# A VectorE product cut in two: when eight multiply-adds run in one piece behind two blocks' low parts

## What is computed

```python
def modulation(cvec, w_mod, b_mod):                  # cvec: 2048, w_mod: 2048 x 12288
    m = jax.nn.silu(cvec) @ w_mod + b_mod            # six vectors of 2048, for c and for c_ctx
    return m.reshape(cvec.shape[0], N_MOD, 1, D_MODEL)

def trunk_layer(x, mod, h0, g, w_in, ...):
    hn = rmsnorm(x, g[0]) * (1.0 + mod[:, 1]) + mod[:, 0]
    z = hn @ w_in                                    # 2048 x 5120
    ...                                              # RG-LRU heads, short convolutions
    x = x + mod[:, 2] * (m @ w_out)
    hn = rmsnorm(x, g[1]) * (1.0 + mod[:, 4]) + mod[:, 3]
    f = (jax.nn.silu(hn @ w_gate) * (hn @ w_up)) @ w_down
    return x + mod[:, 5] * f
```

## Time and profile before

| | before |
|---|---|
| time, median of 3 runs | 1750.77 us (1750.06 to 1751.92) |
| profiled execution, its own time | 1751.09 us |
| its span, first to last instruction | 1749.3 us |
| PE busy | 1710.8 us, 98% of the span |
| DVE busy | 945.4 us, 54% |
| ACT busy | 609.8 us, 35% |
| mean granted clock of PE | 0.992 |

### The profile page before, as it was taken

How to read it: one execution, slowest core, us unless ns; L and a number is a source line. 1 busy time by engine, 2 the same in 40 slices (tenths; PEclk the granted TensorE clock), 3 DMA queues, 4 the chain that set the end, 5 groups by cost and what they waited for, 6 DMA issues and landing times.

```text
span 1749.3 us, 24522 instructions
## 1 busy us (share of the span) xinstructions
PE 1710.8 (98%) x10063; PEld 1632.9 (93%) x10063; DVE 945.4 (54%) x1405; ACT 609.8 (35%) x701; POOL 63.3 (4%) x99
## 2 busy tenths in 40 slices
PE   5999999999999999999999999999999999999997
PEld 3678999999899979999999999999999999999997
DVE  4446678777778578343534434353534435353445
ACT  3333455456523253222222222323232222223235
POOL 2000100110010110000000000000000000000000
PEclk8999999999999999999999999999999999999999
DMA  9996655576677876343334333433333334333421
GB/s 362 379 358 223 239 207 199 201 239 206 212 241 268 289 254 228 121 134 132 120 120 135 129 120 121 136 127 120 121 136 127 120 123 137 124 120 122 141 74 73
DMA packets 206268, 307.56 MB, mean 176 GB/s; under 512 B 5500, under 2 KB 151216, under 8 KB 203776
## 3 DMA queue, kind: packets, MB, share of 16 engines
q1 hardware_dynamic: 189472, 237.07, 40.2%
q0 software_dynamic: 16528, 69.63, 11.1%
q10 hardware_dynamic: 208, 0.02, 0.0%
HBM read 303.55 MB, written 3.15 MB: 175 GB/s over the span
## 4 chain that ended last, share of the span: by engine, by line
PE 94%; DMA 2%; DVE 2%; ACT 1%; issue 0%; SPq 0%; ACTq 0%; DVEq 0%
PE psum L1583 30%; PE psum L1585 29%; PE psum L1584 29%; PE psum L1613 1%; DMA raw<-in_w_mod 1%; DMA scratch<-in_w_in 1%; PE psum L1627 1%; PE psum L1605 1%; PE psum L1638 0%; DVE scratch L1182 0%; PE psum L1920 0%; PE psum L1692 0%; DVE stage L1123 0%; DVE act_lo L1399 0%; ACT scratch L668 0%
## 5 line engine op out<-in xcount | busy, mean ns | idle before, releaser
L967 DVE TENSOR_TENSOR w_lo<-raw,w_hi 128x1024 fp32r<-128x1024 f32 x364 | 444.2, 1224 | 643.3 <-ACT w_hi L633 642.8
L1583 PE MATMUL psum<-act_hi,w_hi 128*128 128x384 f32 x2304 | 775.0, 336 | 5.6 <-DVE act_lo L1139 3.3
L1585 PE MATMUL psum<-act_hi,w_lo 128*128 128x384 f32 x2304 | 770.6, 334 | 0.0
L1584 PE MATMUL psum<-act_lo,w_hi 128*128 128x384 f32 x2304 | 770.4, 334 | 0.0
L633 ACT ACTIVATE w_hi<-raw 128x1024 fp32r<-128x1024 f32 x364 | 381.6, 1058 | 790.8 <-PE psum L1585 718.6
L1583 PEld LDWEIGHTS psum<-act_hi,w_hi 128*128 128x128 f32 x2304 | 432.8, 188 | 35.0 <-issue 25.8
L1584 PEld LDWEIGHTS psum<-act_lo,w_hi 128*128 128x128 f32 x2304 | 433.0, 188 | 0.0
L1585 PEld LDWEIGHTS psum<-act_hi,w_lo 128*128 128x128 f32 x2304 | 432.9, 188 | 0.0
L1583 PE MATMUL psum<-h_hi,w_hi 128*128 128x384 f32 x704 | 235.8, 335 | 0.9 <-DVE h_lo L1443 0.9
L1585 PE MATMUL psum<-h_hi,w_lo 128*128 128x384 f32 x704 | 235.2, 334 | 0.0
L1584 PE MATMUL psum<-h_lo,w_hi 128*128 128x384 f32 x704 | 235.2, 334 | 0.0
(11 more groups left out here) (189 smaller groups left out, 758.4 us busy)
## 6 DMA issues: line engine op xcount, KB each, us to landing
raw<-in_w_mod POOLq DMA_DIRECT2D x50, 1024.0 KB, 6.1
raw<-in_w_gate SPq DMA_DIRECT2D x44, 1024.0 KB, 5.0
raw<-in_w_up SPq DMA_DIRECT2D x44, 1024.0 KB, 5.0
raw<-in_w_down SPq DMA_DIRECT2D x44, 1024.0 KB, 5.0
raw<-in_w_in SPq DMA_DIRECT2D x34, 1024.0 KB, 5.2
raw<-in_w_mod SPq DMA_DIRECT2D x32, 1024.0 KB, 9.4
raw<-in_w_out SPq DMA_DIRECT2D x16, 1024.0 KB, 5.5
stage<-in_w_mod POOLq DMA_DIRECT2D x14, 1024.0 KB, 6.5
```

Of the source, the lines that this page charges most:

```text
L967: dve.tensor_tensor(split_view(w_lo, b), source, split_view(w_hi, b).bitcast(F32), ALU.subtract).then_inc(lo_ready, 1)
L1583: pe.matmul(psum[:, bank, 0:T], hi, x_hi, start=first, stop=False)
L1584: pe.matmul(psum[:, bank, 0:T], hi, x_lo, start=False, stop=False)
L1585: return pe.matmul(psum[:, bank, 0:T], lo, x_hi, start=False, stop=last)
```

## The change

`subtract_beside` puts all eight operations of a unit behind one low part, the second of the two behind which the halves stood.

```diff
             def subtract_beside(kind, n, step, blocks):
 
                 units = SIDE_AT.get(step, ())
-                first = {0: (), 1: (4,), 2: (2, 6), 3: (2, 4, 6)}[len(units)]
+                after = {0: (), 1: (5,), 2: (3, 7), 3: (3, 5, 7)}[len(units)]
                 for b in blocks:
                     subtract_blocks(kind, n, range(b, b + 1))
-                    for unit, at in zip(units, first):
-                        if at <= b < at + 2:
-                            side_half(unit, b - at)
+                    for unit, at in zip(units, after):
+                        if at == b:
+                            side_half(unit, 0)
+                            side_half(unit, 1)
```

## The result

| | before | changed |
|---|---|---|
| time, median of 6 runs | 1750.69 us (1749.65 to 1751.92) | 1758.12 us (1757.52 to 1759.05) |
| ratio | | 1.0042, 95% interval 1.0032 to 1.0052 |
| span of the profiled execution | 1749.3 us | 1756.3 us |

What follows compares the result with a forecast made beforehand. PE, busy 98% of the span, was taken to bound the kernel, just behind a DVE and ACT chain at step ends. Losses of 6.51 + 0.78 = 7.3 us gave 1758.1 us against the median, range 1754.5 to 1761.5.

Steps and rivals of the forecast that it cites:

- the sum: Whole kernel: 6.51 us at steps 2, 5, 6, 7 plus 0.78 in step 8, 7.3 us slower; chance 82%.
- Part 1: Ends of steps 1, 4 to 7: the half moved behind block 7 shifts DVE's chain 2.65 us against PE.
- The rooms: PE's room at block 1: 1.10 us in steps 2 and 5, 1.51 in step 6, 0.62 in step 7.
- the four forecasts: PE's losses at the starts of steps 2, 5, 6, 7: 1.61, 1.61, 1.20, 2.09 us.
- the upper bound: Ten slow matmul starts at blocks 0 and 1 add 1.2 us, a late later block up to 2.1: 1761.7 us.
- The lower bound: Four step starts: only block 0's room counts and block 1 catches up, taking 2.5 us off: 1755.6 us.
- Step 8: First activation low part: the 2.65 us shift, less 1.79 idle and 0.08 overlap, costs PE 0.78 us.
- Part 2 and 3: Halves moved behind blocks 3 and 5, and the load queues of SP and POOL: no cost, no gain.
- The four operations' price: Four operations ahead of subtract_gates take 2.65 us by the row; 2.98 by the skill would give 1759.8 us.
- Absorbed: Step ends: sooner loads and high parts start the chain sooner, so not slower, 1751 us; chance 9%.
- Faster: Loads issued sooner relieve PE, gaining at most 2.3 us, 1748.5 us; chance 3%.
- The clock: PE's clock falls in the new waits at five places, 4 us more, 1762.4 us; chance 6%.

Runs made afterwards that it cites:

- the repeat: The changed kernel itself measured once more, nothing edited: 1759.15 us against the first kernel's 1751.01, ratio 1.0047.
- whole behind 6: Changed kernel with the second unit of steps 1 and 4 to 7 whole behind block 6 instead of 7: 1750.91 us, ratio 0.9998.
- the first experiment: Changed kernel with only units behind block 3 (and 5) whole, those behind block 7 back in halves behind blocks 6 and 7: 1751.09 us, ratio 1.0002.
- the later copy: Changed kernel, second units whole behind block 6, and step 8's copy_row moved behind the first three activation low parts: 1750.31 us, ratio 0.9996.
- whole behind 7: Kernel before, with only the second unit of steps 1 and 4 to 7 whole behind block 7: 1759.18 us, ratio 1.0048.
- steps 2 and 3 behind 7: Kernel before, with the single units of steps 2 and 3 whole behind block 7: 1759.14 us, ratio 1.0046.
- four more: Kernel before, halves unmoved, plus four operations ahead of subtract_gates in steps 1 and 4 to 7: 1762.75 us, ratio 1.0067.

## Why the prediction was right, point by point

**The forecast** was 1758.1 us and the measurement 1758.12; the sum was 7.3 us and the trace's five losses 7.7. So close an agreement of the medians is partly luck: the repeat came out at 1759.15, its five losses were again 7.7 to 7.8, and one stretch of the program moves by 1 us and more between executions.

**Part 1, the shift.** 2.65 us per step end, tied to PE at its start: shown, by the idle time of ACT (5.17 to 7.83 us) with its wait for PE unchanged at 2.72, and by the kernel with four added operations, which loses by the same rule with nothing moved. That it is the place and not the run of eight is shown by the two kernels without loss (whole behind 3, whole behind 6).

**The rooms.** The step names and the four forecasts hold to 0.13 us each, all a little low. The missing part is the slow start after a wait, which the sum had left for the upper bound: with 0.08 us at each of four step ends it would have read 7.6. The upper bound's 0.12 us at ten starts, 1.2 us, was too much by about 0.8.

**Where PE waits.** I spoke of the loss as one at block 1. PE waits at block 0 first and for the remaining 0.6 us at block 1, because DVE's low parts 0 and 1 are 4.78 us apart (233.44 to 238.22) and PE's blocks only 4.16. The total is set by block 1, as forecast. The waits that I had put at 1 to 2 us each are in fact two per step end, 0.8 to 1.7 us together. The lower bound of 1755.6, in which only block 0 counted, is ruled out by these waits.

**Step 8.** 0.78 us forecast, 0.77 lost; DVE's 1.79 us of idle time ahead of line 1006 took the rest of the shift.

**Part 2 and 3.** The swaps behind blocks 3 and 5 and the sooner loads cost and gained nothing: shown by the first experiment. POOL issued the load of the unit for step 2 at 229.27 us, which is 230.05 in the time of the first trace, as forecast. But the search for the smallest room, blocks 0 and 1 in the prediction, was incomplete. It did no harm there, since the rooms at block 2 of the four steps were larger (before, 3.3, 2.7, 3.3 and 2.2 us); it did in the expectation for steps 3 and 4.

**The four operations' price.** The row's 2.65 us decided against the estimate of 2.98 us that I worked out by what the Trainium skill, "VectorE: DVE Perf Modes", section "The DRAIN you can't avoid", says of held operations. The run of eight agrees with the row: from 223.59 to 228.90 are 5.31 us, 0.66 each, so these operations overlap.

**The rivals.** Absorbed: ACT would have had to begin sooner, and it waited for PE 2.72 us as before. Faster: the first experiment has the sooner loads and no gain. The clock: it did not fall in the new waits. The windows around the largest of them, in steps 7 and 8, read 1.00 (the third value from the end; the earlier trace rows has the order), and so do those at steps 2, 5 and 6:

```profile
428.00:440.00 12.00, 10.32 (x61) 9.12 (x54) 10.87 (x17) 9.06 (x10) 0.75 (x1) 1.00 0.67 237
464.00:486.00 22.00, 18.95 (x114) 17.04 (x113) 20.77 (x29) 14.60 (x17) 1.50 (x2) 1.00 0.51 160
```

It did fall elsewhere, in a stretch near 620 to 630 us where it falls in the first kernel too; the last section tells of it.

## What to carry to other kernels

Before moving work on an engine that looks half idle, follow its next steps to the bottleneck engine and note the room at each handover: the loss is the shift less the smallest room, and the smallest may be some blocks behind the edit. Idle time counts only at the place where it lies: here 4.9 us of it stood one instruction ahead of a chain with 0.6 to 1.5 us to spare, and moving 2.65 us of work across that instruction cost 1.3 to 2.2 us at each of four step ends and 0.8 at the fifth. When two traces are compared, compare distances from a common event, not times.

## What the runs showed of the hardware that I had not expected

**A thin stretch of PE takes a different time in different executions.** Between the last block of `w_out` and the first of `w_gate` PE has short matmuls and small waits. Against the execution of before, PE's lag changes there by -0.75 us (whole behind 3, and the later copy), by 0.1 us or less (the change's first trace, and four others) or by +1.1 to +1.4 us (whole behind 7, steps 2 and 3 behind 7, four more, and the change once more). The same two matmuls of 128x384, in the first kernel, and in the one with the later copy:

```profile
618.44 1.65 PE L1936 MATMUL psum<-token_rows,ones 128*128 128x384 f32 x2 [0.33 <-DVE token_rows L1470]
```

```profile
617.87 0.91 PE L1938 MATMUL psum<-token_rows,ones 128*128 128x384 f32 x2 [0.33 <-DVE token_rows L1472]
```

The windows of 610 to 650 us (us, busy PE, PEld, DVE, ACT, POOL, then PEclk, the granted clock) of the first kernel, of the later copy, and of the change once more:

```profile
610.00:650.00 40.00, 39.67 (x255) 30.37 (x254) 31.92 (x53) 24.33 (x34) 5.25 (x7) 0.96 0.65 225
```

```profile
610.00:650.00 40.00, 39.01 (x260) 30.80 (x259) 31.92 (x53) 24.45 (x34) 5.26 (x7) 1.00 0.68 238
```

```profile
610.00:650.00 40.00, 39.93 (x248) 30.73 (x247) 28.65 (x51) 19.45 (x28) 4.49 (x6) 0.91 0.78 276
```

All twelve traces sort by this number: 1.00 in the two at -0.75 us, 0.96 in the first kernel and the five near 0, 0.91 in the four at +1.1 to +1.4. By estimate, 0.96 over 40 us is some 3 us at the lower of the two levels, 1.2 GHz, and 0.91 some 7 us. The changed kernel has 0.96 in one execution and 0.91 in the other, so the program alone does not decide it. Whether a late PE makes the longer spell likelier is open: of the five traces in which PE comes some 7 us or more late to this place four have it, of the seven others none. About 1 us of the loss that the runs measure may come from it; the 7.7 us at the five places do not. For a change of 1 us in this kernel, the block ends in the trace tell more than medians do.

**An operation that waits for the one just before it.** Four `scalar_tensor_tensor` of 128x512 took 3.15 us when each waited for its predecessor, and 2.65 us in the side unit, where each waits for the one before the last: 0.12 us apiece. The four read and write other tiles than the unit does, and no run here separates the two.
